# Attention's products in plain float32, two heads on halves of the array

## The reference, cut to what matters

```python
s = jnp.einsum('bqghd,bngd->bghqn', q_c, kc) * scale         # compressed
p_cmp = masked_softmax(s, valid) * any_valid
o_cmp = jnp.einsum('bghqn,bngd->bqghd', p_cmp, vc)
...                                                          # selected: ks, vs; window: kw, vw
p = masked_softmax(jnp.einsum('bqghd,bkgd->bghqk', q_c, kwc) * scale, mask_w)
o_win = jnp.einsum('bghqk,bkgd->bqghd', p, vwc)
return g_c[..., 0:1] * o_cmp + g_c[..., 1:2] * o_slc + g_c[..., 2:3] * o_win
```

## Time and profile before

| | |
|---|---|
| median of 3 runs (lowest, highest) | 1786.74 us (1786.24, 1787.28) |
| the profiled execution | 1785.22 us, of which 1783.4 from the first to the last instruction |
| TensorE busy | 1764.0 us, 99% |
| weight loads busy | 1462.5 us, 82% |
| VectorE busy | 856.6 us, 48% |
| ScalarE busy | 592.8 us, 33% |
| attention, from the first step of `j` = 0 to the last values | about 528 to 633 us of the span |

### The profile page before, as it was taken

How to read it: one execution, slowest core, us unless ns; L and a number is a source line. 1 busy time by engine, 2 the same in 40 slices (tenths; PEclk the granted TensorE clock), 3 DMA queues, 4 the chain that set the end, 5 groups by cost and what they waited for, 6 DMA issues and landing times.

```text
span 1783.4 us, 22116 instructions
## 1 busy us (share of the span) xinstructions
PE 1764.0 (99%) x8132; PEld 1462.5 (82%) x8132; DVE 856.6 (48%) x1100; ACT 592.8 (33%) x832; POOL 86.5 (5%) x81
## 2 busy tenths in 40 slices
PE   8999999999999999999999999999999999999999
PEld 6888888877878888888888888888888888888887
DVE  5544443347788845444443344444432554444322
ACT  5333332234336634333322233333222433333211
POOL 0500000012000010000000000000001000000000
PEclk9999999999999999999999999999999999999999
DMA  6333333352320023333343323333332233333331
GB/s 178 95 94 96 103 111 96 88 130 60 94 71 13 1 67 99 95 94 94 95 127 93 96 84 95 98 101 94 113 97 67 77 106 95 94 94 112 109 97 48
DMA packets 321362, 163.68 MB, mean 92 GB/s; under 512 B 13893, under 2 KB 320041, under 8 KB 321322
## 3 DMA queue, kind: packets, MB, share of 16 engines
q1 hardware_dynamic: 321130, 163.08, 31.9%
q10 hardware_dynamic: 192, 0.08, 0.0%
HBM read 161.04 MB, written 2.10 MB: 91 GB/s over the span
## 4 chain that ended last, share of the span: by engine, by line
PE 93%; DVE 3%; ACT 2%; issue 1%; DMA 0%; SPq 0%; POOL 0%; DVEq 0%; ACTq 0%
PE ps_s L532 20%; PE ps_s L533 20%; PE ps_s L534 20%; PE ps_y L532 9%; PE ps_y L534 9%; PE ps_y L533 9%; PE ps_aux L862 1%; DVE w_lo L1392 1%; ACT w_hi L1014 1%; DVE scratch L1404 1%; ACT scratch L1270 0%; PE ps_y L845 0%; DMA x_in<-in_x 0%; PE ps_s L813 0%; DVE small L1746 0%
## 5 line engine op out<-in xcount | busy, mean ns | idle before, releaser
L1392 DVE TENSOR_TENSOR w_lo<-raw,w_hi 128x1024 fp32r<-128x1024 f32 (+1 forms) x275 | 365.3, 1328 | 725.2 <-ACT w_hi L1014 725.0
L532 PE MATMUL ps_s<-xg_hi,w_hi 128*128 128x512 f32 x1576 | 617.9, 392 | 0.1
L534 PE MATMUL ps_s<-xg_hi,w_lo 128*128 128x512 f32 x1576 | 613.4, 389 | 0.0
L533 PE MATMUL ps_s<-xg_lo,w_hi 128*128 128x512 f32 x1576 | 613.3, 389 | 0.0
L1014 ACT CAST w_hi<-raw 128x1024 fp32r<-128x1024 f32 (+1 forms) x275 | 307.9, 1119 | 583.1 <-PE ps_y L534 291.7
L532 PEld LDWEIGHTS ps_s<-xg_hi,w_hi 128*128 128x128 f32 x1576 | 295.9, 188 | 67.1 <-DVE w_lo L1392 2.8
L533 PEld LDWEIGHTS ps_s<-xg_lo,w_hi 128*128 128x128 f32 x1576 | 295.9, 188 | 62.4 <-issue 1.7
L534 PEld LDWEIGHTS ps_s<-xg_hi,w_lo 128*128 128x128 f32 x1576 | 295.9, 188 | 61.9
L532 PE MATMUL ps_y<-act_hi,w_hi 128*128 128x512 f32 x704 | 274.3, 390 | 0.7 <-DVE w_lo L1392 0.7
L534 PE MATMUL ps_y<-act_hi,w_lo 128*128 128x512 f32 x704 | 273.9, 389 | 0.0
L533 PE MATMUL ps_y<-act_lo,w_hi 128*128 128x512 f32 x704 | 273.9, 389 | 0.0
(11 more groups left out here) (310 smaller groups left out, 1035.8 us busy)
## 6 DMA issues: line engine op xcount, KB each, us to landing
raw<-in_ffn_w_gate SPq DMA_DIRECT2D x88, 512.0 KB, 3.9
raw<-in_ffn_w_up SPq DMA_DIRECT2D x88, 512.0 KB, 3.9
raw<-in_ffn_w_down SPq DMA_DIRECT2D x64, 704.0 KB, 4.6
raw<-in_hyb_w_in SPq DMA_DIRECT2D x19, 512.0 KB, 3.8
x_in<-in_x SPq DMA_DIRECT2D x8, 256.0 KB, 6.0
w_raw<-in_hyb_cmp_w SPq DMA_DIRECT2D x4, 512.0 KB, 6.8
raw<-in_hyb_w_in SPq DMA_DIRECT2D x8, 256.0 KB, 3.8
raw<-in_hyb_w_out SPq DMA_DIRECT2D x16, 128.0 KB, 2.9
```

The source lines that it names most:

```text
L532: mm(bank, hi, x_hi, start=first, stop=False, **kw)
L533: mm(bank, hi, x_lo, start=False, stop=False, **kw)
L534: return mm(bank, lo, x_hi, start=False, stop=last, **kw)
L1392: tt(w_lo[:, n % 2, 0:size], raw[:, n % 4, 0:size], f32(w_hi[:, n % 2, 0:size]), ALU.subtract).then_inc(lo_ready, 1)
```

## The change

- The scores are plain float32 products of 64 rows: the stationary operand is `qf` itself, the moving one `keys`, both on the partitions of the head's group. A step `s` now has branch `br = s // 4` and query block `c = s % 4`, and does both groups' heads: `g` = 0 on rows 0 to 63 of the array, `g` = 1 on rows 64 to 127, each into its bank. Widths are exactly `(c + 1) * 128`.
- The values take 64 columns of `v_t` for each head, and write the head's 64 partitions of `ps_aux`; the two heads alternate. One accumulation now goes over both branches; the compressed part is added with the second branch, at its end.
- The splits of queries and keys, with their buffers and semaphores, are gone. `split_output` and `output_low` run twice for each `j`, on all 128 partitions.
- `j` = 1 and 2 are written out on all engines; the hardware loop is gone.
- `ptc` holds both heads; `w2_hi` and `w2_lo` get buffers of their own.

```diff
             def scores(j, s):
...
-                g, c = s // 4, s % 4
+                br, c = s // 4, s % 4
                 width = (c + 1) * P
-                pe.wait_ge(qp_lo_ready, 2 * j + g + 1)
+                if s == 0:
+                    pe.wait_ge(rope_ready, head_tiles("q3" if j == 3 else "kc"))
                 at_least(pe, exp_done, 8 * j + s - 1)
...
-                for br in range(2):
-                    bank = ps_s[:, 2 * (s % 2) + br, :]
-                    mm(bank[:, 0:wide], query, k_hi[:, br, g, 0:wide], start=False, stop=False, skip_group_check=True)
-                    last_mm = mm(bank[:, 0:wide], query, k_lo[:, br, g, 0:wide], start=False, stop=True,
-                                 skip_group_check=True)
+                for g in range(2):
+                    rows_ = slice(g * DH, (g + 1) * DH)
+                    last_mm = mm(ps_s[:, 2 * (s % 2) + g, 0:width], qf[rows_, j * T + c * P:j * T + (c + 1) * P],
+                                 keys[rows_, br, 0:width], start=False, stop=True, skip_group_check=True)
                 last_mm.then_inc(qk_done, 1)
 
             def scores_c(j, g):
...
-                    mm(bank, query, kc_hi[:, g, :], start=False, stop=False)
-                    last_mm = mm(bank, query, kc_lo[:, g, :], start=False, stop=c == NQ - 1)
+                    last_mm = mm(ps_stat[:, c * NCP:(c + 1) * NCP], qf[rows_, j * T + c * P:j * T + (c + 1) * P],
+                                 keys_c[rows_, g * NCP:(g + 1) * NCP], start=False, stop=c == NQ - 1)
...
             def values(j, pair):
...
-                pe.wait_ge(c_pt_ready, 2 * j + pair // 2 + 1)
-                at_least(pe, o_lo_ready, 4 * j + pair)
-                mm(bank, vc_t[:, :], ptc[:, queries], start=True, stop=False)
-                for br in range(2):
-                    for k in range(2 * half_pair + 1):
-                        mm(bank, v_t[:, br, k * P:(k + 1) * P], probs[:, br, k, :, :], start=False, stop=False)
-                    k = 2 * half_pair + 1
-                    last_mm = mm(bank[:, P:2 * P], v_t[:, br, k * P:(k + 1) * P], probs[:, br, k, 1, :], start=False, stop=br == 1)
+                br, half_of = pair // 2, pair % 2
+                queries = slice(half_of * 2 * P, (half_of + 1) * 2 * P)
+                heads = [ps_aux[g * DH:(g + 1) * DH, queries] for g in range(2)]
...
+                if pair in (0, 3):
+                    at_least(pe, o_lo_ready, 2 * j + pair // 3)
+                for k in range(2 * half_of + 1):
+                    for g in range(2):
+                        mm(heads[g], values_of(g, k), probs[:, g, k, :, :], start=pair == 0 and k == 0, stop=False,
+                           skip_group_check=True)
+                k = 2 * half_of + 1
+                for g in range(2):
+                    last_mm = mm(heads[g][:, P:2 * P], values_of(g, k), probs[:, g, k, 1, :], start=False, stop=False,
+                                 skip_group_check=True)
+                if br == 1:
+                    pe.wait_ge(c_pt_ready, 2 * j + 2)
+                    for g in range(2):
+                        last_mm = mm(heads[g], vc_t[:, g * DH:(g + 1) * DH], ptc[:, g, queries], start=False, stop=True,
+                                     skip_group_check=True)
                 last_mm.then_inc(pv_done, 1)
...
-            with pe.Fori(1, 3) as j:
+            for j in (1, 2):
                 attend(j)
...
-            def split_output(j, pair):
...
+            def split_output(j, half_of):
+                act.wait_ge(pv_done, 4 * j + half_of + 3)
+                at = j * T + half_of * 2 * P
+                copy(o_hi[:, at:at + 2 * P], ps_aux[:, half_of * 2 * P:(half_of + 1) * 2 * P]).then_inc(o_hi_ready, 1)
...
             def attend(j, first=False, last=False):
                 for s in range(8):
-                    if s % 2 == 0 and not (first and s <= 2):
-                        split_output(j, (s - 4) // 2)
+                    if s in (0, 2) and not first:
+                        split_output(j - 1, s // 2)
...
-                    if s in (3, 7) and not last:
-                        split_query(j + 1, s // 4)
...
-            project_four(3, 0, {0: kc_norm, 1: kc_rope, 2: kc_low})
+            project_four(3, 0, {0: kc_norm, 1: kc_rope})
```

More of the change, by code:

```diff
@@ L248, in build @@
             small_c = mb("small_c", [P, 5, NQ])
-            w2_hi, w2_lo = (q_parts[:, i, 0:2 * P].rearrange("p (c d) -> p c d", c=2) for i in range(2))
+            keys_c = mb("keys_c", [P, 2 * NCP])
         with ExitStack() as pool_ctx:
@@ L916, in _ @@
             from_conv(1)
[L917 removed]
+            pe.wait_ge(o_lo_ready, 8)
             from_attention(0)
@@ L1151, in square @@
                 nc.scalar.activation(dst, src, ACT.Square).then_inc(head_sq, 1)
-            def split_keys(br):
-                act.wait_ge(rope_ready, head_tiles("ks") + br)
-                for g in range(2):
-                    for h in range(2):
-                        last = copy(k_hi[h * DH:(h + 1) * DH, br, g, :], work[g * DH:(g + 1) * DH, br, :])
-                last.then_inc(k_hi_ready, 1)
             def odd_keys(c):
@@ L1183, in kc_square, with take_values_c @@
                 nc.scalar.activation(kcm[:, 0, :], square_in, ACT.Square).then_inc(head_sq, 1)
-            def kc_split():
-                act.wait_ge(rope_ready, head_tiles("kc"))
-                for g in range(2):
-                    last = copy(kc_hi[:, g, :], kcv[:, 0, g * NCP:(g + 1) * NCP])
-                last.then_inc(kc_hi_ready, 1)
+            def take_values_c():
                 act.wait_ge(aux_done, AUX.index("t_vc") + 1)
@@ L1268, in exps @@
                 act.wait_ge(negmax_ready, 8 * j + s + 1)
-                for br in range(2):
-                    last = nc.scalar.activation(prob_of(s)[:, br * T:br * T + width], ps_s[:, 2 * (s % 2) + br, 0:width],
-                                                ACT.Exp, bias=small[:, s % 2, br:br + 1],
-                                                accum_out=small[:, s % 2, 2 + br:3 + br])
+                for g in range(2):
+                    last = nc.scalar.activation(prob_of(s)[:, g * T:g * T + width], ps_s[:, 2 * (s % 2) + g, 0:width],
+                                                ACT.Exp, bias=small[:, s % 2, g:g + 1],
+                                                accum_out=small[:, s % 2, 2 + g:3 + g])
                 last.then_inc(exp_done, 1)
@@ L1323, in _ @@
             attend(0, first=True)
-            with act.Fori(1, 3) as j:
+            for j in (1, 2):
                 attend(j)
             attend(3, last=True)
-            split_output(3, 2)
+            split_output(3, 0)
             take_probs(3, 7)
-            split_output(3, 3)
+            split_output(3, 1)
             for d in range(KD):
@@ L1554, in rope @@
                 tt(dst, dst, m1[:, :], ALU.add).then_inc(rope_ready, 1)
-            def keys_low(br):
-                dve.wait_ge(k_hi_ready, br + 1)
-                for g in range(2):
-                    rows_ = slice(g * DH, (g + 1) * DH)
-                    for h in range(2):
-                        last = tt(k_lo[h * DH:(h + 1) * DH, br, g, :], work[rows_, br, :], f32(k_hi[rows_, br, g, :]),
-                                  ALU.subtract)
-                last.then_inc(k_lo_ready, 1)
             def pairs_of(n, p, c):
@@ L1805, in attend @@
                         convolved_low(3, work[:, 0, :])
-                    if s % 2 == 0 and not (first and s <= 2):
-                        output_low(j, (s - 4) // 2)
+                    if s in (0, 2) and not first:
+                        output_low(j - 1, s // 2)
                     if not (first and s == 0):
@@ L1813, in attend @@
                         scales_c(j, s // 4)
-                    if s in (3, 7) and not last:
-                        query_low(j + 1, s // 4)
                     if first and s == 3:
```

116 lines of the change are left out of this document (32 added, 84 removed).

## The result

| | before | changed |
|---|---|---|
| median (lowest, highest) | 1786.68 us, measured beside it | 1769.82 us (1769.16, 1770.43) |
| ratio, 95% interval | | 0.9907 (0.9895 to 0.992) |
| the profiled execution | 1785.22 us, span 1783.4 | 1770.43 us, span 1768.6 |

The change saves 16.9 us by the medians, 14.8 us between the two profiled executions. I had forecast 4.5 us more and a range from 1777: both miss.

A forecast was written before the change was run, and what follows sets the result against it. TensorE was taken to bound the kernel, narrowly ahead of VectorE. Terms +1.55 - 4.6 + 4.0 + 0.3 gave +1.25 us a block, four blocks +5.0, less 0.5: forecast 1791 us, own range 1786 to 1797, whole range 1777 to 1815.

The forecast's parts named there:

- scores: Attention scores as plain 64-row products for each head: +1.55 us a block, bounds -0.8 and +3.5.
- 2T: Lower bound for a score step's four records, T being one record's time (0.11 to 0.43 us): -0.8 us a block.
- values: Value products of two heads side by side on column halves: -4.6 us a block, bounds 0 and -5.2.
- changes of division: 24 switches a block between whole and half array: 0.12 us behind a mask, 0.2 otherwise, +4.0 us a block, at most 7.
- waits: TensorE's waits in an attention block, raised from 1.0 to 1.3 us because the long value groups are shorter.
- products start in program order: In score steps, order A1, A2, B1, B2 for heads A and B: B1 runs beside A2, 6.45 us a block.
- 3T: A score step takes three record times T if the row halves run side by side and products start in order.
- Worth nothing directly: VectorE's work falling from 21.5 to 19.3 us a block saves no time directly, since TensorE covers it.
- The way in: Between projections and attention: VectorE loses 1.4 us of splits, TensorE gains 1.1 us of work; about 0, or -1.2.
- Exposed loads: Rival: B's weight load starts only with A2, 2.9 us a block less 0.3 of waits, 1801 us; chance 0.21.
- no overlap: Rival: plain float32 halves run one after another, 7.0 us a block more, 1814 us; chance 0.21.
- changes cheap: Rival: array division switches at half price give 1783 us (chance 0.10), free ones 1776 (0.11); together 0.21.

The follow-up runs named there:

- the two experiments: Each against the changed kernel: both heads' scores on the same array rows, 1787.57 us; value products over the whole array instead of column halves, 1787.97 us.

## Why the prediction was wrong, point by point

The forecast was +1.25 us a block; the block lost 3.6. By its own terms:

| us a block | forecast | measured | |
|---|---|---|---|
| scores | +1.55 | -0.8 | 2T, the lower bound named |
| values | -4.6 | -5.2 | the lower bound named |
| changes of division | +4.0 | +3.2 | |
| waits | +0.3 | about -0.8 | what is left over |
| sum | +1.25 | -3.6 | 25.1 to 21.54: -3.6 |

The waits before were the 1.0 by which the sum of products fell short of the block. In the same way 0.2 is left after: scores 4.3, values 5.2, transpositions 4.4, masks 1.4, the compressed branch 2.8 and changes 3.2 are 21.3 of 21.54. So this term is a remainder on both sides, not a wait read from a view.

**The step that failed first: "products start in program order".** From it came 3T for the scores and one T more for each group of values. The records show 2T: a half starts its first pass beside the other half's first, past a second pass that stands between them in the order. This is 2.35 us a block at the scores and 0.6 at the values, 3.0 of the 4.9 by which the block was missed; 0.8 more is in the changes of division and 1.1 in the waits. I had both bounds in the text and took the middle by a reason that no row bore out. The row that could have told was not there: before, no two halves were at work.

**Changes of division: the mechanism was right, the larger size was off.** A change shows twice in the records: nothing starts for 0.09 us after the product before it has streamed, and then the first product's weight load is exposed. In the step above the second mask starts at 552.015 and streams for 0.056, and the scores start at 552.164: 0.09. Their first passes take 552.697 - 552.164 = 0.53 where a pass streams for 0.43: 0.10 for the load. The second passes have streamed by 553.13, and line 852 starts at 553.22: 0.09 again. Its first pass takes 553.490 - 553.223 = 0.27 where a pass streams for 0.215: 0.05 for the load. So a change behind a mask costs 0.20, of which the price of the masks held 0.06 before: 0.13 more, and I had taken 0.12. A change out of scores or values costs 0.15, and out of the compressed scores, which start only every 0.11 us anyway, 0.1; I had taken 0.2 for all. That is 1.3 for the ten ways into rows (forecast 1.2), 1.3 for the ten out (2.0) and 0.6 for the four behind values (0.8): 3.2. The two rare products from which I took 0.2 stood beside 512-column work, as the prediction says. The Trainium skill (TensorEngine Tiling, Key Properties) says that a change of tiling mode drains TensorE, and the late starts and loads at lines 804, 852 and 832 agree, at 0.09 us.

**Waits and VectorE.** I raised the waits from 1.0 to 1.3, and about 0.2 is left of them. "Worth nothing directly" held in mid-attention: with VectorE's work put back, a block takes 21.55 us. It did not hold at the start, where TensorE does wait for VectorE: 1.2 us there. So VectorE's relief isn't what lowered the waits within a block, and what did stays open. The two halves of the change still help each other: with the splits kept, TensorE's gain ends in waits (4.6 us in all), by where the splits stand more than by their load. The forecast of VectorE's own time, 19.3, was right.

**What held.** The price of a record, 0.215 for 256 columns and 0.43 for 512, carried over to the halves unchanged. The price of a change behind a mask held too. The way in: I said about 0, and TensorE's first mask behind the projections' scaling stands at 528.46 us where it stood at 528.37. The compressed scores keep their distance of 0.11 (eight records, 549.62 to 550.42 from the first to the last start).

**The rivals.** Exposed loads and no overlap are out: `A` and `B` load and stream together. Had nothing overlapped, the kernel would stand at about 1803 by adding the two experiments (an estimate), not 1814. The rival on the other side, changes cheap, named the right side of the result for a wrong reason: with 3T and free changes it gave 1776, still above what came. The Trainium skill (TensorE: Matmul & The Clock Gate, Packing small matmuls) reports tiles that overlap almost fully; the trace agrees, 1.06 us for two scores that take 1.91 on the same rows. In the prediction I let it speak against two rivals, but kept 3T, which it spoke against as well. The range should have reached to the sum of all lower bounds.

## What to carry to other kernels

Products on different halves of the array run at once if neither waits for the other; alternate them finely, since a half gets only about four passes ahead of its turn. Price a change of division at 0.09 us of standing still plus the first weight load behind it (0.05 us for 64 columns, 0.10 for 128 columns on half the rows, in float32), whatever stands before it, and look for neighbouring steps that could share a division before joining steps that others wait for. When a change relieves a second engine, put that engine's work back without its waits: here the load cost nothing in mid-attention, and the waits tied to the splits cost the time. And when bounds are wide, let the range reach the sum of the bounds on each side.

## What the runs showed of the hardware that was not expected

- Two products on the row halves start 6 to 7 ns apart (552.164 and 552.170), although a pass of the first stands between them. With one head's eight passes in front, the other's first waits for the fifth to start (552.680 behind 552.674).
- Work of different steps mixes on the halves without any hint in the program: with masks on the row halves, the next step's mask (line 802) starts at 550.12, ahead of the last two compressed scores (line 818, 550.23 and 550.34).
- In the two kernels where one overlap was taken away, TensorE's granted clock fell for some 4 to 8 us of the profiled execution. The stages (columns as in the earlier trace rows) of the scores on the same rows, and of the values over the whole array:

```profile
520.00:524.00 4.00, 4.00 (x26) 3.09 (x25) 3.80 (x8) 0.64 (x4) 0.00 (x0) 1.00 0.49 135
524.00:528.00 4.00, 4.00 (x11) 2.93 (x10) 1.36 (x4) 1.39 (x7) 0.00 (x0) 0.58 0.00 0
```
```profile
532.00:536.00 4.00, 2.88 (x19) 1.75 (x18) 3.93 (x11) 3.35 (x11) 0.00 (x0) 0.86 0.00 0
536.00:540.00 4.00, 4.00 (x15) 2.73 (x14) 3.73 (x8) 1.65 (x5) 0.00 (x0) 0.50 0.00 0
```

A clock of 0.50 is the lower of the two levels, 1.2 GHz. In the first case TensorE had been busy for the whole stage before, in the second for 2.88 of 4 us. The changed kernel's profiled execution has 1.00 in all these stages, and its work there is nearly the same. What brings it about is open. Other kernels had single executions with a mean clock of 0.997 too (1773.22 with two products in turn, 1773.25 with masks on rows and compressed scores joined). With the scores on the same rows eight of ten executions were below 1.0, and their median stands 2.5 us above the two at full clock.
